# Weights in units of two groups: 1 MB transfers and operations of 2048 columns, with rings of two units

## The reference, cut to what matters

```python
for layer in range(DEPTH):                      # 2
    h = rms_norm(x, norm_w[layer])
    proj = jnp.einsum('bsd,de->bse', h, w_in[layer])
    (g_q, g_k, g_v, g_a, s_q, s_k, s_v, d_q, d_k, d_v, r_x, gate) = split_cols(proj, IN_SPLITS)
    y = jnp.concatenate([gla_mixer(...), swa_mixer(...), diff_mixer(...), rglru_mixer(...)], axis=-1)
    y = y * jax.nn.silu(gate)
    x = x + jnp.einsum('bse,ed->bsd', y, w_out[layer])
```

## Time and profile before

| | us |
|---|---|
| median of 3 runs | 2905.15 (2905.13 to 2905.78) |
| the profiled execution | 2904.84 |
| its span, first to last instruction | 2903.1 |
| TensorE busy | 2892.3 (100%) |
| TensorE's weight loads | 2373.4 (82%) |
| VectorE busy | 1576.7 (54%) |
| ScalarE busy | 1445.9 (50%) |
| DMA, mean | 188 GB/s |

### The profile page before, as it was taken

How to read it: one execution, slowest core, us unless ns; L and a number is a source line. 1 busy time by engine, 2 the same in 40 slices (tenths; PEclk the granted TensorE clock), 3 DMA queues, 4 the chain that set the end, 5 groups by cost and what they waited for, 6 DMA issues and landing times.

```text
span 2903.1 us, 34721 instructions
## 1 busy us (share of the span) xinstructions
PE 2892.3 (100%) x13461; PEld 2373.4 (82%) x13461; DVE 1576.7 (54%) x2080; ACT 1445.9 (50%) x2053; POOL 66.2 (2%) x106
## 2 busy tenths in 40 slices
PE   9999999999999999999999999999999999999999
PEld 7878888888888888888888888888888888888887
DVE  6545555555667455444554455555556664554444
ACT  6344454555656555444554344455555665553333
POOL 2000000000000000000000000000000000000000
PEclk9999999999999999999999999999999999999999
DMA  8655556565655666666666555565656566666665
GB/s 255 195 163 177 170 170 189 179 186 175 182 160 175 188 196 196 215 218 203 217 198 181 172 167 181 175 186 171 191 177 182 160 178 181 201 202 205 227 221 165
DMA packets 282965, 546.49 MB, mean 188 GB/s; under 512 B 17752, under 2 KB 22496, under 8 KB 282800
## 3 DMA queue, kind: packets, MB, share of 16 engines
q1 hardware_dynamic: 272560, 524.88, 58.6%
q0 software_dynamic: 5552, 17.26, 2.0%
q10 hardware_dynamic: 4688, 2.13, 0.3%
HBM read 535.81 MB, written 8.39 MB: 187 GB/s over the span
## 4 chain that ended last, share of the span: by engine, by line
PE 99%; ACT 0%; issue 0%; DVE 0%; DMA 0%; SPq 0%; ACTq 0%
PE main L1129 93%; PE mixer L1129 4%; PE mixer L1351 0%; PE mixer L1169 0%; PE mixer L1157 0%; PE mixer L1284 0%; PE mixer L1327 0%; DMA w_raw<-in_w_in 0%; PE mixer L1312 0%; PE mixer L1200 0%; PE mixer L1274 0%; PE mixer L1311 0%; ACT w_hi L376 0%; DVE w_lo L703 0%; PE mixer L1230 0%
## 5 line engine op out<-in xcount | busy, mean ns | idle before, releaser
L1129 PE MATMUL main<-w_hi,act 128*128 128x512 f32 x7936 | 2522.3, 394 | 2.0 <-ACT stage L386 0.9
L703 DVE TENSOR_TENSOR w_lo<-w_raw,w_hi 128x1024 fp32r<-128x1024 f32 x992 | 1207.0, 1227 | 1092.9 <-ACT w_hi L376 1086.2
L1129 PEld LDWEIGHTS main<-w_hi,act 128*128 128x128 f32 x7936 | 1490.9, 188 | 323.9 <-DVE w_lo L703 4.5
L1129 PE MATMUL main<-w_lo,act 128*128 128x512 f32 x3968 | 1545.8, 390 | 0.0
L376 ACT ACTIVATE w_hi<-w_raw 128x1024 fp32r<-128x1024 f32 x992 | 1041.4, 1058 | 966.8 <-PE main L1129 909.4
L1129 PEld LDWEIGHTS main<-w_lo,act 128*128 128x128 f32 x3968 | 746.4, 188 | 148.1
L386 ACT ACTIVATE act_T<-main,rstd 128x512 f32<-128x512 f32 x28 | 19.1, 682 | 68.2 <-PE main L1129 68.2
L683 DVE SCALAR_TENSOR_TENSOR act<-act_T,par,act 128x256 fp32r<-128x256 f32 x96 | 42.0, 479 | 15.2 <-ACT act L358 15.1
L386 ACT ACTIVATE stage<-main,rstd 128x512 f32<-128x512 f32 x40 | 27.3, 684 | 38.3 <-PE main L1129 37.7
L386 ACT ACTIVATE mix_Y<-main,rstd 128x512 f32<-128x512 f32 x24 | 16.4, 682 | 59.2 <-PE main L1129 59.2
L933 DVE TENSOR_TENSOR mix<-mix,main 128x512 f32<-128x512 f32 x32 | 22.0, 688 | 42.6 <-PE main L1129 42.6
(11 more groups left out here) (225 smaller groups left out, 1016.8 us busy)
## 6 DMA issues: line engine op xcount, KB each, us to landing
w_raw<-in_w_in SPq DMA_DIRECT2D x736, 512.0 KB, 3.7
w_raw<-in_w_out SPq DMA_DIRECT2D x256, 512.0 KB, 3.6
out<-mix POOLq DMA_DIRECT2D x15, 512.0 KB, 3.2
mix<-in_x POOLq DMA_DIRECT2D x8, 512.0 KB, 5.9
mix<-out POOLq DMA_DIRECT2D x8, 512.0 KB, 5.9
mix_Y<-in_x SPq DMA_DIRECT2D x7, 512.0 KB, 6.9
act_T<-in_lru_w_r ACTq DMA_DIRECT2D x16, 64.0 KB, 1.7
act_T<-in_lru_w_i ACTq DMA_DIRECT2D x16, 64.0 KB, 2.0
```

What stands on the lines that cost most here:

```text
L703: dve.tensor_tensor(w_lo[:, n % LO, :, :], w_raw[:, n % RAW, :, :], w_hi[:, n % HI, :, :].bitcast(F32), ALU.subtract).then_inc(w_lo_ready, 1)
L1129: return pe.matmul(out_, lhsT, rhs, start=start, stop=stop, skip_group_check=True)
```

## The change

Weights are handled in units of two groups. Of the three rings of four groups each becomes a ring of two units in the same memory. `weights`, `hi` and `lo` do their work only for even g, for groups n and n + 1 together: one transfer of 1 MB, one rounding and one difference of 2048 columns. `w_landed` has one semaphore per unit; `w_hi_ready` and `w_lo_ready` count units. A unit's rounding and difference wait for `w_used` of n - 2, which is that both groups of the unit before the last are used; its transfer waits for the difference of that unit. TensorE still raises `w_used` after each group. The first transfers on SP's queue are put in another order. TensorE's matmuls, the mixers and their places in the iterations stay.

```diff
-    RAW, HI, LO = 4, 4, 4
+    RING = 4
...
             def weights(layer, j, g):
                 n = group(layer, j, g)
-                rows = slice(g * KG * P, (g + 1) * KG * P)
+                rows = slice(g * KG * P, (g + 2) * KG * P)
...
-                if n >= RAW:
-                    sp.wait_ge(w_lo_ready, n - RAW + 1)
-                sp.dma_start(w_raw[:, n % RAW, :, :], src.rearrange("(k p) n -> p k n", p=P)
-                             ).then_inc(w_landed[n % RAW], 16)
+                if n >= RING:
+                    sp.wait_ge(w_lo_ready, (n - RING) // 2 + 1)
+                slot = n % RING
+                sp.dma_start(w_raw[:, slot:slot + 2, :, :].rearrange("p s k n -> p (s k) n"),
+                             src.rearrange("(k p) n -> p k n", p=P)).then_inc(w_landed[slot // 2], 16)
...
             x_piece(0)
+            x_piece(1)
             weights(0, 0, 0)
-            x_piece(1)
-            weights(0, 0, 1)
             x_piece(2)
             x_piece(3)
+            x_piece(4)
             weights(0, 0, 2)
-            x_piece(4)
-            weights(0, 0, 3)
...
-                        if n >= RAW:
+                        if n >= RING and g % 2 == 0:
                             weights(layer, j, g)
...
             def hi(layer, j, g):
                 n = group(layer, j, g)
-                act.wait_ge(w_landed[n % RAW], 16 * (n // RAW + 1))
-                if n >= HI:
-                    act.wait_ge(w_used, n - HI + 1)
-                act.activation(w_hi[:, n % HI, :, :], w_raw[:, n % RAW, :, :],
-                               ACT.Copy).then_inc(w_hi_ready, 1)
+                slot = n % RING
+                if g % 2 == 0:
+                    act.wait_ge(w_landed[slot // 2], 16 * (n // RING + 1))
+                    if n >= RING:
+                        act.wait_ge(w_used, n - RING + 2)
+                    act.activation(w_hi[:, slot:slot + 2, :, :], w_raw[:, slot:slot + 2, :, :],
+                                   ACT.Copy).then_inc(w_hi_ready, 1)
...
             def lo(layer, j, g):
                 n = group(layer, j, g)
-                dve.wait_ge(w_hi_ready, n + 1)
-                if n >= LO:
-                    dve.wait_ge(w_used, n - LO + 1)
-                dve.tensor_tensor(w_lo[:, n % LO, :, :], w_raw[:, n % RAW, :, :],
-                                  w_hi[:, n % HI, :, :].bitcast(F32), ALU.subtract).then_inc(w_lo_ready, 1)
+                slot = n % RING
+                if g % 2 == 0:
+                    dve.wait_ge(w_hi_ready, n // 2 + 1)
+                    if n >= RING:
+                        dve.wait_ge(w_used, n - RING + 2)
+                    dve.tensor_tensor(w_lo[:, slot:slot + 2, :, :], w_raw[:, slot:slot + 2, :, :],
+                                      w_hi[:, slot:slot + 2, :, :].bitcast(F32), ALU.subtract).then_inc(w_lo_ready, 1)
...
-                        pe.wait_ge(w_lo_ready, n + 1)
+                        pe.wait_ge(w_lo_ready, n // 2 + 1)
```

More of the change, by code:

```diff
@@ L75, in hybrid_trunk @@
         YB = sb("mix_Y", [P, T * D])
-        w_raw = sb("w_raw", [P, RAW, KG, NC])
-        w_hi = sb("w_hi", [P, HI, KG, NC], F32R)
-        w_lo = sb("w_lo", [P, LO, KG, NC], F32R)
+        w_raw = sb("w_raw", [P, RING, KG, NC])
+        w_hi = sb("w_hi", [P, RING, KG, NC], F32R)
+        w_lo = sb("w_lo", [P, RING, KG, NC], F32R)
         stage = sb("stage", [P, T, NC])
@@ L156, in hybrid_trunk @@
         par_turned, par_chain, par_exp_in, par_exp = sem("par_turned"), sem("par_chain"), sem("par_exp_in"), sem("par_exp")
-        w_landed = [sem(f"w_landed{s}") for s in range(RAW)]
+        w_landed = [sem(f"w_landed{s}") for s in range(RING // 2)]
         w_hi_ready, w_lo_ready, w_used = sem("w_hi_ready"), sem("w_lo_ready"), sem("w_used")
@@ L1133, in chunk_group @@
                 n = group(layer, j, g)
-                hi, lo = w_hi[:, n % HI, :, :], w_lo[:, n % LO, :, :]
+                hi, lo = w_hi[:, n % RING, :, :], w_lo[:, n % RING, :, :]
                 for t in range(T):
```

## The result

The changed kernel takes 2966.91 us (median of 4 runs, 2966.31 to 2967.59), the kernel before 2905.47 us beside it (4 runs, 2905.13 to 2906.01): the ratio is 1.0212, with a 95% interval of 1.0198 to 1.0227. That is 61.4 us more, where 67 were predicted, and inside the range. The profiled execution took 2966.31 us, its span is 2964.6.

A forecast was written before the change was run, and what follows sets the result against it. TensorE's train of 992 groups of 12 matmuls was taken to bound the kernel. Terms 6.3 + 12.1 + 17.4 + 12.0 + 8.0 + 4.8 + 6.5 = 67 us, added to 2904.84, gave 2972; 8-in-10 range 2938 to 3022.

The forecast's parts named there:

- restarts: TensorE matmuls released by a difference: 0.06 us more for each of some 109 stalls, 6.5 us.
- The lead: Plain units: ready 4.59 us after TensorE began the one before, against 5.44; lead falls from 5.6 to 0.85 us, hidden.
- Inside a sliding-window chunk: 16 chunks: late 0.14 at the start, 0.4 before turns, 0.75 before products, 0.2 regained; net 1.09 us each, 17.4.
- GLA chunks: Eight chunks: next chunk's first unit 1.05 us late six times, 2.1 twice in a layer's last; sum 12.1 us.
- The 0.2 us in iteration 4: GLA chunks: iteration 4 sends its gate to TensorE 0.2 us late, eight times.
- Differential and gate chunks: Differential: 0.4, 0.3 (q and k copy) and 0.85 late, 12.0 us; gate: 2 x (0.4 + 1.15 + 1.15 + 1.3) = 8.0.
- The start: First matmul at about 13.5 us instead of 8.58, +4.9; chunk 0's split late in four units, 1.4; sum 6.3.
- The transfers: 1 MB transfers hidden, except 0.3 us in each of 16 chunks with x on POOL's queue: 4.8 us.
- The landing: 1 MB weight transfer: 5.3 us from issue to landing, against 3.7 for 512 KB; other bound 7.4.
- The late transfer: Rival, chance 0.18: 1 MB takes 7.4 us, stalls of 0.5 to 0.8 at some 60 places, +40 us: 3012.
- Not slower: Rival, chance 0.10: lead enough nearly everywhere if wide rounding and difference together take at most 3.05 us; about 2905.
- The clock rival: Rival, chance 0.06: TensorE's clock falls in about 60 stalls above 0.4 us, 2 us each, 120: 3090.

The follow-up runs named there:

- Experiment 3: Changed kernel with each rounding and difference made as two of 1024 columns, TensorE waiting for its half; 1 MB units kept: 2922.12 us, ratio 1.0057.
- Experiment 4: Kernel before with rings of three groups instead of four for w_hi and w_lo, operations and transfers as before: 2917.32 us, ratio 1.0041.
- Experiment 5: Changed kernel with sliding-window exponentials ahead of iteration 10's rounding and the copy of turned probabilities ahead of iteration 12's difference: 2946.43 us, ratio 1.0143.
- experiment 10: Kernel before with 1 MB transfers for every unit but the first, which comes in two halves in the old start order: 2905.27 us, ratio 1.0000.
- experiment 2: Changed kernel with transfers taken back to 512 KB and the old queue order at the start; wide operations kept: 2964.66 us, ratio 1.0204.
- experiment 1: Kernel before with 1 MB transfers and the changed kernel's start order; roundings, differences and TensorE's waits stay at one group: 2909.28 us, ratio 1.0014.
- experiment 8: Kernel before with the rounding of group 1 ahead of the evacuation of the first half, in chunks 1 to 23: 2906.07 us, ratio 1.0003.
- experiment 9: Kernel before with group 1's rounding ahead of the first half's evacuation only in chunks 1, 9 to 16 and 21 to 23: 2900.09 us, ratio 0.9981.
- experiment 6: Changed kernel with its first unit alone brought, rounded and differenced as two halves, in the old queue order: 2963.53 us, ratio 1.0195.
- experiment 7: Changed kernel with halved roundings and differences, sliding-window exponentials and copy put ahead, and first unit in halves; 1 MB units kept: 2908.93 us, ratio 1.0013.

## Why the prediction was right, point by point

**The total.** The walk found the right mechanism, and its total is also helped by luck. The terms came to 67.1 us; without the falls of the clock, for which there was no term, they measured 56.4. Had the clock held, the forecast would have been some 11 us too high instead of 5.6. The largest misses are GLA (3.9) and the 6.5 for restarts: the restarts are there, but the values found hold them, so the waits themselves were walked too long by about as much. One of the prediction's own signs of being wrong did show, a clock below 1 (0.998 as the mean of the core).

**The lead.** Right. The widths are 1.91 and 2.29 us, as taken; plain chunks lose nothing; and the loss lies at the jobs that keep an engine longer than 0.85 us from its next unit. Experiment 3 is the test: narrow operations and TensorE's wait by group give back 45 us, with the transfers and the ring's room as changed. Experiment 4 separates the two parts of the lead: a ring shorter by one group, with narrow operations, costs the mixers nothing. What the change loses is thus mostly the time of the wide pieces themselves and the tie of a group to its neighbour (which of the two was not tested apart), more than the room in the ring.

**Inside a sliding-window chunk.** Right, term for term. Walked: 1.09 us and the restarts, about 1.27; found: 1.16. By the starts of the matmuls in both traces, the chunk loses 0.16 at group 2, 0.43 before the turns and 0.75 before the products, and regains 0.20 in group 0, where 0.14, 0.4, 0.75 and 0.2 were walked. The weight loads before the turns and the products show 0.64 and 0.91 of idle time, the matmuls 0.22 and 0.49. Since a weight load may begin before the matmuls in front of it have ended, the idle time of its queue is more than what is lost. Experiment 5 shows that the cause is the order behind a wide operation: nothing else was moved.

**GLA chunks.** Too high by 3.9 us. The ends of the first two chunks of a layer cost 1.0 each, as walked. The end of the third costs about 0.1: TensorE has 1.03 us of turns for the recurrent part to do behind group 14 of chunk 6, and the rounding gains their time. That I had not walked. The rows are the weight load behind the second GLA chunk, these turns, and the weight load behind the third:

```profile
306.81 0.19 PEld L1135 LDWEIGHTS main<-w_hi,act 128*128 128x128 f32 x1 [1.12 <-DVE w_lo L709]
...
353.24 1.03 PE L1206 MATMUL mixer<-ident,stage 128*128 128x128 f32 x8
...
356.81 0.19 PEld L1135 LDWEIGHTS main<-w_hi,act 128*128 128x128 f32 x1 [0.23 <-DVE w_lo L709]
```

The end of the last costs 2.0, where 2.1 were walked. The 0.2 us in iteration 4 do not exist.

**Differential and gate chunks.** The first 1.23 to 1.38 against 1.5, the second 0.46, 1.22, 1.18 and 1.05 against 0.4, 1.15, 1.15 and 1.3: right in the main. By the starts of the matmuls a differential chunk loses 0.44 before the first head's turns and 0.87 at its end, as walked; the 0.3 us for the copy of q and k do not exist.

**The start.** The walk was right, its landing was not. The first rounding begins at 9.93 us, 1.5 later than I took from the bytes ahead of it:

```profile
9.93 1.91 ACT L379 ACTIVATE w_hi<-w_raw 128x2048 fp32r<-128x2048 f32 x1 [7.24 <-DMA w_raw<-in_w_in]
...
15.09 0.77 PE L1135 MATMUL main<-w_hi,act 128*128 128x512 f32 x1 [8.37 <-DVE act L695]
```

The first matmul is 6.5 us later than before instead of the 4.9 walked, and chunks 0 and 1 add 0.7 instead of 1.4: the split was late in two of the four units (0.39 each), not in all.

**The transfers.** The size of the term, 4.8, was met by the 4.9 found in w_out, but by luck: it was walked as 0.3 in each of 16 chunks, and what was found stands mostly at four places. With narrow operations the large transfer costs nothing (experiment 10), 512 KB transfers do not mend chunk 24 (experiment 2), and narrow operations do (experiment 3). Of 3.94 us in that one chunk, 2.35 are a hole behind a unit whose bytes came late, and 1.6 the clock. That transfer, issued at 1184.07, took 10.1 us, while POOL's queue stored and loaded x and brought parameters and 256 KB of w_in for the next layer. Its landing, then ScalarE, VectorE and TensorE twice:

```profile
DMA to landing us min/median/max: 10.1/10.1/10.1
...
1194.26 1.92 ACT L379 ACTIVATE w_hi<-w_raw 128x2048 fp32r<-128x2048 f32 x1 [5.47 <-DMA w_raw<-in_w_out]
...
1196.21 2.29 DVE L709 TENSOR_TENSOR w_lo<-w_raw,w_hi 128x2048 fp32r<-128x2048 f32 x1 [6.46 <-ACT w_hi L379]
...
1198.56 0.50 PE L1135 MATMUL main<-w_hi,act 128*128 128x512 f32 x1 [2.10 <-DVE w_lo L709]
...
1200.27 1.06 PE L1135 MATMUL main<-w_hi,act 128*128 128x512 f32 x2
```

From bytes to the first matmul lie 4.3 us of wide operations; the narrow ones need 2.3. Two more units of w_out in layer 1, whose roundings also waited for their bytes, cost 0.30 and 0.42. The fourth place has nothing to do with transfers: TensorE loses 1.5 us at the start of layer 1. There VectorE's addition that frees the accumulator stands behind a split of activations (L686), and that behind a wide difference. The first row is of the kernel before, where the addition starts 1.06 us before the matmul that needs it, at 1461.41; the others are VectorE twice and the waiting matmul of the changed kernel:

```profile
1460.35 0.69 DVE L933 TENSOR_TENSOR mix<-mix,main 128x512 f32<-128x512 f32 x1 [1.01 <-PE main L1129]
...
1493.85 1.67 DVE L686 SCALAR_TENSOR_TENSOR act<-act_T,par,act 128x256 fp32r<-128x256 f32 x4
1495.43 1.51 DVE L939 TENSOR_TENSOR mix<-mix,main 128x512 f32<-128x512 f32 x2
...
1496.26 0.47 PE L1135 MATMUL main<-w_hi,act 128*128 128x512 f32 x1 [1.23 <-DVE mix L939]
```

Experiments 1 and 10 lose nothing there, experiment 3 loses 0.8, and experiment 4, with narrow operations and a shorter ring, the same 1.5. So this loss is the lead's, and here the room in the ring counts too.

**The landing.** Issue to landing is 4.8, 5.1 and 12.6 us (minimum, median, maximum), where 512 KB had 3.2, 3.7 and 9.9; I took 5.3. The Trainium skill (DMA: Bandwidth & Descriptors, Anatomy of one DMA) makes it 4.4, an estimate from its fit for the software queue; the trace of this hardware queue has 5.1, and the second half megabyte costs 1.4 instead of the 1.2 estimated from that page.

**The rivals.** The late transfer is refuted at its size: the landing takes 5.1 us and not 7.4, and with narrow operations it costs TensorE nothing beyond the start (experiments 1 and 10). With wide ones late bytes cost 3.1 us at three places of w_out instead of 40 us. "Not slower" is refuted by the widths: 4.21 us together, where it needed 3.05. The clock rival is true in small: it put 2 us at each of 60 stalls, and the clock fell at three, for 1.6 us each. The forecast had put it at nothing; it is told below.

## What to carry to other kernels

Count the lead of a producer in time, as the room in the ring less the whole length of its piece of work, and compare it with the longest job that may stand in front of that piece. Merging two roundings and two differences here saved 162 us of busy time of two engines that idle half the time and cost 61 us of the engine that sets the end. Where a wide operation cannot be avoided, what the bound engine waits for goes in front of it (some 17 us here), and it can be had for nothing where the queue idles anyway; but the same move does harm where the engine arrives late, so it is placed chunk by chunk, which is what made experiments 8 and 9 differ by 6 us.

## What the runs showed of the hardware

**The clock fell after some holes of about 2 us.** In the changed kernel TensorE's granted clock dropped to 1.2 GHz three times, for some eight matmuls, and each time right behind a hole. These are two stretches of 6 us at the same place of the two layers, each beginning inside a hole of 2.17 us, one where the clock held and one where it fell (busy time and count of PE, PEld, DVE, ACT and POOL, then the granted clock, the DMA share and GB/s):

```profile
408.00:414.00 6.00, 5.25 (x23) 4.37 (x24) 4.04 (x6) 2.31 (x3) 0.00 (x0) 1.00 0.53 175
...
1881.00:1887.00 6.00, 5.69 (x18) 4.55 (x19) 4.05 (x7) 2.30 (x3) 0.00 (x0) 0.72 0.54 175
```

The matmuls behind such a hole come 0.43 us apart instead of 0.23 (the row at 1200.27 above: 1.06 less 0.63). It costs 1.6 us a time: chunk 8 grows by 1.85 us in layer 0, where the clock held, and by 3.43 in layer 1, where it fell; chunk 23 by 1.05 and 2.63. In the profiled executions of the changed kernel and of experiments 2, 5 and 6 there were, behind the start, 20 holes of 1.77 to 2.53 us in the stream of matmuls, and 10 of them were followed by the lower clock (3, 2, 1 and 4). It is not settled by the length: behind the hole of 2.16 or 2.17 us after the last GLA chunk of layer 0 the clock fell in experiment 6 and held in the three others, and of two holes of 2.53 us, at the same place of experiments 2 and 6, it fell behind one. It never fell behind the four holes of 1.23 to 1.25 us, nor behind any of the shorter ones in experiments 1, 3 and 7, whose mean granted clock is 1.000. The Trainium skill (TensorE: Matmul & The Clock Gate, A second HAM failure mode) tells of another kernel, in which short idle times between groups of matmuls come often enough that the clock swings between its two levels; the trace agrees that short holes can bring a fall, 3 times in the changed kernel, and here they were single holes. What decides between holding and falling stays open. So a hole of 2 us has to be priced at up to 3.6 us.

**The width of an operation is nearly all rate.** From 1024 to 2048 columns ScalarE's rounding goes from 1058 to 1914 ns and VectorE's difference from 1227 to 2292: the merging saves 202 and 162 ns a unit, in pieces that were hidden.
